# Expert weights in 1 MB chunks of 8 KB runs instead of 2 MB chunks of 16 KB runs

## The reference

```python
def moe_ffn(h, w_router, b_router, w_gu, b_gu, w_down, b_down):
    logits = jnp.matmul(h, w_router, preferred_element_type=F32) + b_router
    top_val, top_e = lax.top_k(logits, TOP_K)              # 4 of 32 experts
    gates = jax.nn.softmax(top_val, axis=-1)
    ...                                                     # tokens sorted by expert
    def expert_block(a):
        xi, e = a
        gate, up = jnp.split(xi @ w_gu[e] + b_gu[e], 2, axis=-1)
        gate = jnp.minimum(gate, SWIGLU_LIMIT)
        up = jnp.clip(up, -SWIGLU_LIMIT, SWIGLU_LIMIT)
        act = (up + 1.0) * gate * jax.nn.sigmoid(SWIGLU_ALPHA * gate)
        return act @ w_down[e] + b_down[e]
    ...                                                     # weighted sum per token
```

## Time and profile before

| What | Value |
|---|---|
| Median of 3 runs | 1431.72 us (1431.07 to 1437.1) |
| Profiled execution, its own time | 1433.07 us |
| Its span (first to last instruction) | 1431.3 us |
| TensorE, busy | 1312.5 us (92%), granted clock 0.982 |
| DVE, ACT, POOL, busy | 437.7, 230.6, 239.6 us |
| Moved by DMA | 482.73 MB, mean 337 GB/s |
| w_gu and w_down | 128 + 64 transfers of 2 MB, 21.9 and 22.4 us from issue to landing (median) |

### The profile page before, as it was taken

One profiled execution on the slowest core, in us unless ns is written; L12 is line 12 of the kernel. 1 busy time (PEld: TensorE's weight loads), 2 busy tenths in 40 slices (PEclk: granted clock), 3 DMA queues, 4 the chain that ended last, 5 costly groups with the idle time before them and its releaser, 6 DMA issues.

```text
span 1431.3 us, 22343 instructions
## 1 busy us (share of the span) xinstructions
PE 1312.5 (92%) x8102; PEld 643.8 (45%) x8102; DVE 437.7 (31%) x853; ACT 230.6 (16%) x537; POOL 239.6 (17%) x477
## 2 busy tenths in 40 slices
PE   7999688999889799999999999998999999899994
PEld 5787565677646333333333333333333333233331
DVE  2124544323431622223232232321232323222226
ACT  1124434120320201001111011110010101100102
POOL 4000000000001312212212122121131221121302
PEclk9999899999999899999999999999999999999997
DMA  9435339525589399999999999999999999999991
GB/s 255 151 106 181 118 115 323 194 101 182 196 331 412 142 394 415 421 415 428 429 431 429 402 425 430 431 430 429 431 419 429 430 430 430 430 424 422 430 430 70
DMA packets 73542, 482.73 MB, mean 337 GB/s; under 512 B 5146, under 2 KB 38098, under 8 KB 48658
## 3 DMA queue, kind: packets, MB, share of 16 engines
q1 hardware_dynamic: 71346, 475.29, 81.6%
q0 software_dynamic: 2064, 6.10, 1.2%
q10 hardware_dynamic: 48, 0.13, 0.0%
HBM read 475.84 MB, written 5.64 MB: 336 GB/s over the span
## 4 chain that ended last, share of the span: by engine, by line
PE 83%; DMA 7%; issue 3%; DVE 3%; ACT 2%; POOL 0%; SPq 0%; ACTq 0%; DVEq 0%; POOLq 0%; PEldq 0%
PE bank L1074 27%; PE bank L546 10%; PE bank L1113 10%; DMA mem<-in_w_gu 5%; PE bank L1023 5%; PE bank L1013 5%; PE bank L555 4%; PE bank L1117 3%; PE bank L533 3%; PE bank L1028 3%; PE bank L967 2%; PE bank L1016 2%; DMA mem<-in_w_in 1%; PE bank L1104 1%; PE bank L1036 1%
## 5 line engine op out<-in xcount | busy, mean ns | idle before, releaser
L1074 PE MATMUL bank<-mem 128*32 128x256 f32 (+1 forms) x3136 | 424.3, 480 | 11.6 <-DMA mem<-in_w_gu 10.4
L1074 PEld LDWEIGHTS bank<-mem 128*32 128x32 f32 (+1 forms) x3136 | 155.7, 121 | 258.9 <-issue 199.6
L2351 DVE TENSOR_TENSOR mem<-mem,bank 128x512 f32<-128x512 f32 (+1 forms) x180 | 114.2, 684 | 406.2 <-PE bank L1013 405.1
L1485 ACT ACTIVATE mem<-bank 128x512 f32<-128x512 f32 (+7 forms) x236 | 110.5, 496 | 549.6 <-PE bank L1113 159.0
L1113 PE MATMUL bank<-mem 128*64 128x512 f32 x672 | 153.5, 598 | 15.4 <-issue 15.4
L546 PE MATMUL bank<-mem 128*128 128x288 f32 (+1 forms) x640 | 158.7, 405 | 4.7 <-PE bank L546 3.3
L546 PEld LDWEIGHTS bank<-mem 128*128 128x128 f32 x640 | 121.4, 192 | 39.9 <-issue 8.4
L1426 POOL COPY mem<-mem 96x64 bf16 x35 | 8.7, 249 | 613.0 <-PE bank L1096 612.7
L1803 ACT ACTIVATE mem<-mem 128x512 f32<-128x512 f32 (+1 forms) x35 | 19.1, 545 | 527.3 <-DVE mem L2365 527.3
L1113 PEld LDWEIGHTS bank<-mem 128*64 128x64 f32 x672 | 48.8, 136 | 90.6 <-issue 90.6
L2285 DVE TENSOR_TENSOR mem<-bank,vec 128x512 f32<-128x512 f32 x36 | 24.9, 692 | 206.0 <-PE bank L1036 206.0
(11 more groups left out here) (248 smaller groups left out, 984.3 us busy)
## 6 DMA issues: line engine op xcount, KB each, us to landing
mem<-in_w_gu SPq DMA_DIRECT2D x128, 2048.0 KB, 21.9
mem<-in_w_down SPq DMA_DIRECT2D x64, 2048.0 KB, 22.4
mem<-in_w_in SPq DMA_DIRECT2D x12, 1024.0 KB, 9.9
mem<-in_w_mkv SPq DMA_DIRECT2D x8, 1024.0 KB, 9.6
mem<-in_cache_k SPq DMA_DIRECT2D x16, 512.0 KB, 7.1
mem<-in_cache_v SPq DMA_DIRECT2D x16, 512.0 KB, 5.5
mem<-in_cache_mem_k SPq DMA_DIRECT2D x8, 1024.0 KB, 4.8
mem<-in_cache_mem_v SPq DMA_DIRECT2D x8, 1024.0 KB, 5.4
```

The lines of the kernel that those rows point to most:

```text
L1074: last = pe.matmul(to, ebias[0:96, 0:kind] if k is None else xgT[:, k, 0:kind], columns(src, j, t, kind), **flags)
L1485: return act.activation(out, in_, ACT.Copy, scale=scale)
L2351: dve.tensor_tensor(a, a, ps, ALU.add).then_inc(added, 1)
```

## The change

Chunks are halved: eight of w_gu (128 rows, one row of 8 KB per partition) and four of w_down (256 rows, two rows per partition), in twenty slots of 1 MB in the same ten places. Both halves of one of the first ten places are issued one behind the other. PE waits for and gives back each half by itself. With one row of w_gu per partition the contraction's blocks are plain blocks of 128 rows, so the reordering around it goes: `gather` reads blocks of 128 columns and has six products of 512 columns in place of four of 512 and four of 256; the second copy of scale and shift with its four transfers goes; narrow passes read and write in one run; the activation's transposes read in another order. `combine` stands behind the fifth block in place of the sixth.

```diff
-GU_CHUNKS, DN_CHUNKS = 4, 2
+GU_CHUNKS, DN_CHUNKS = 8, 4
-ALL = 10
+ALL = 20
-SLOT = 4096
+SLOT = 2048
...
-            at = HOME + PLACES[i % ALL] * SLOT
+            at = HOME + PLACES[i // 2 % len(PLACES)] * 2 * SLOT + i % 2 * SLOT
...
         def gu_src(e, k):
-            return A["w_gu"][0, bass.ds(e, 1), 256 * k:256 * k + 256, :].rearrange("a (p r) n -> p (a r n)", p=P)
+            return A["w_gu"][0, bass.ds(e, 1), P * k:P * k + P, :].rearrange("a p n -> p (a n)")
         def dn_src(e, j):
-            return A["w_down"][0, bass.ds(e, 1), 512 * j:512 * j + 512, :].rearrange("a (p r) n -> p (a r n)", p=P)
+            return A["w_down"][0, bass.ds(e, 1), 256 * j:256 * j + 256, :].rearrange("a (p r) n -> p (a r) n", p=P)
...
-                for c in range(2):
+                for c in range(3):
                     for h in range(2):
-                        pe.matmul(bank[0][64 * h:64 * h + 64, :], pick[:, c, :], z[:, c, :].rearrange("p (q h) -> p h q", h=2)[:, h],
-                                  start=(c == 0), stop=False)
-                for odd in range(2):
-                    for h in range(2):
-                        to = bank[0][64 * h:64 * h + 64, :].rearrange("p (b o x) -> p o b x", b=4, o=2)[:, odd]
-                        last = pe.matmul(to, pick[0:64, 2 + odd, :], z2.rearrange("p (b x h) -> p h b x", b=4, h=2)[:, h],
-                                         start=False, stop=(odd == 1))
+                        if c < 2:
+                            token, rows = pick[:, c, :], z[:, c, :].rearrange("p (b h x) -> p h b x", b=4, h=2)[:, h]
+                        else:
+                            token, rows = pick[0:64, 2 + h, :], z2
+                        last = pe.matmul(bank[0][64 * h:64 * h + 64, :], token, rows, start=(c == 0), stop=(c == 2))
...
-                    if k == 2:
+                    if k == 4:
                         pe.wait_ge(y_ready, n + 1)
                         pe.wait_ge(selT_ready, n + 1)
                         pe.wait_ge(added, n * 5 + 1)
                         combine()
...
-            for name, at in (("ln2_g", 40), ("ln2_b", 48)):
-                for h in range(2):
-                    pool.dma_start(vec_rows[at + 4 * h:at + 4 * h + 4, :], A[name][0].rearrange("(a p h) -> h a p", p=P, h=2)[h],
-                                   allow_slow_non_contiguous=True).then_inc(vec_in, 16)
```

More of the change, by code:

```diff
@@ L190, in chunk_slot @@
         def chunk_slot(i):
-            at = HOME + PLACES[i % ALL] * SLOT
+            at = HOME + PLACES[i // 2 % len(PLACES)] * 2 * SLOT + i % 2 * SLOT
             return mem[:, at:at + SLOT]
         def at_place(place, at, *shape):
-            return carve(mem, HOME + place * SLOT + at, *shape)
+            return carve(mem, HOME + place * 2 * SLOT + at, *shape)
         aT = carve(mem, 0, KB, T)
@@ L1065, in expert_pass @@
                 parts, width = P // kind, D * kind // P
-                def products(src, k, **flags):
+                pe.wait_ge(xg_ready, n + 1)
+                for k in range(KB):
+                    w = chunk_arrived(group, q, k)
                     for j in range(2):
                         for t in range(parts):
-                            to = bank[1 + j][kind * t:kind * t + kind, 0:width]
-                            if kind != CAP:
-                                to = to.rearrange("p (x v) -> p x v", v=2)
-                            last = pe.matmul(to, ebias[0:96, 0:kind] if k is None else xgT[:, k, 0:kind], columns(src, j, t, kind), **flags)
-                    return last
-                pe.wait_ge(xg_ready, n + 1)
-                for k in range(GU_CHUNKS):
-                    w = chunk_arrived(group, q, k)
-                    for r in range(2):
-                        last = products(w[:, 2 * D * r:2 * D * r + 2 * D], 2 * k + r, start=(k + r == 0), stop=(k == GU_CHUNKS - 1 and r == 1))
-                    if k < GU_CHUNKS - 1:
+                            last = pe.matmul(bank[1 + j][kind * t:kind * t + kind, 0:width], xgT[:, k, 0:kind],
+                                             w[:, D * j + width * t:D * j + width * t + width], start=(k == 0), stop=(k == KB - 1))
+                    if k < KB - 1:
                         last.then_inc(chunk_used, 1)
-                    if k == 1:
-                        pe.wait_ge(bias_ready, n + 1)
-                        products(bgu, None, start=False, stop=False)
-                    if k == 2:
+                    if k == 4:
                         pe.wait_ge(y_ready, n + 1)
@@ L1091, in expert_pass @@
                         combine()
+                    if k == 3:
+                        pe.wait_ge(bias_ready, n + 1)
+                        for j in range(2):
+                            for t in range(parts):
+                                pe.matmul(bank[1 + j][kind * t:kind * t + kind, 0:width], ebias[0:96, 0:kind],
+                                          bgu[:, D * j + width * t:D * j + width * t + width], start=False, stop=False)
                 last.then_inc(gu_done, 1)
@@ L1101, in expert_pass @@
                 pe.wait_ge(act_ready, n + 1)
-                by_row = act_s[:, 0:width].rearrange("p (x r) -> p r x", x=P)
+                by_row = act_s[:, 0:width].rearrange("p (i x r) -> p i r x", x=P, r=2)
                 for j in range(width // P):
-                    last = pe.transpose(bank[3][:, P * j:P * j + P], by_row[:, j, :], C("ident"))
+                    last = pe.transpose(bank[3][:, P * j:P * j + P], by_row[:, j // 2, j % 2, :], C("ident"))
                 last.then_inc(act_turned, 1)
@@ L1176, in chunk, with first_chunk @@
                 j = i % CHUNKS_E
-                src = gu_src(e, j) if j < GU_CHUNKS else dn_src(e, j - GU_CHUNKS)
-                sp.dma_start(chunk_slot(i), src).then_inc(slot_in[i % ALL], 16)
-            def first_chunk(i):
-                chunk(i // CHUNKS_E, i)
+                dst, s = chunk_slot(i), slot_in[i % ALL]
+                if j < KB:
+                    sp.dma_start(dst, gu_src(e, j)).then_inc(s, 16)
+                else:
+                    sp.dma_start(dst.rearrange("p (r n) -> p r n", r=2), dn_src(e, j - KB)).then_inc(s, 16)
+            def first_chunk(place):
+                for i in (2 * place, 2 * place + 1):
+                    chunk(i // CHUNKS_E, i)
             for i, item in enumerate(ITEMS):
@@ L1596, in _ @@
             last.then_inc(read_sem(("vs",)), 1)
-            carry(("vec",), vec[:, :], wide(56))
+            carry(("vec",), vec[:, :], wide(40))
             act.wait_ge(keys_stored, 16 * 2)
```

39 lines of the change are left out of this document (18 added, 21 removed).

## The result

| | before | after |
|---|---|---|
| median of 9 runs each on one chip | 1432.32 us (1431.07 to 1437.1) | 1424.95 us (1418.97 to 1426.37) |
| profiled execution (span) | 1433.07 us (1431.3) | 1421.8 us (1420.0) |

The ratio of the two kernels over all these runs is 0.993, with a 95% interval of [0.9915, 0.9946]; that of the two medians is 0.9949. The time of 1424.95 lies in the forecast range of 1424 to 1439, but the forecast was "no change" (1429.5, chance 0.66), and "faster" had 0.14.

A forecast was written before the change was run, and what follows sets the result against it. The expert stage was taken as bound by PE, then the weight stream, then PE. Terms +4.9 - 1.1 - 2.46 - 3.0 - 0.6 = -2.3 us; from the median of 1431.72 the forecast was 1429.5 us, range 1424 to 1439.

The forecast's parts named there:

- the start: Kernel start: four single-word gathers leave the POOL queue, removing PE's 0.58 us wait for first weights; -0.6 us.
- stream, 8 KB runs: Expert weights from 814.86 to 1236.49: 8 KB runs cost 0.059 us more per old chunk, 83 chunks, +4.9 us.
- halves (1.1 and 2.46): Stream-bound piece: earlier return of space near 814.86 saves 1.1 us; PE starting on the first half at its end saves 2.46.
- the combine's place: Expert passes: combine moves one block ahead; its input is ready since the pass before, so nothing new is waited for.
- gather: Next tokens' gather: 0.15 us shorter in thirteen passes before 814.86 and seven behind 1236.49; -3.0 us.
- narrow reading: Narrow experts' products: one run instead of pairs costs nothing, 0.060 us per 256 columns in both.
- issues of SP: Sign of being right: SP issues of 1 MB take about the old time each.
- the stall at 814.86: Expert stage: the stream last found no place here; before it PE alone was taken to set the time.
- The slow stream: Rival, expert weights: 8 KB runs pay the 4 KB price, 0.175 us per chunk; 1439, chance 0.2 with all else slower.
- the transfers in a row: Rival, expert weights: transfers do not overlap, so 2.7 us latency adds to each of 364 halves; 2410, chance 0.01.
- The runs cost nothing: Rival, expert weights: 8 KB runs cost 0 per chunk and the gather gains its best; 1421, chance 0.14.
- The down source: Rival, down weights: runs stay 4 KB there, so the stream costs 8.1 us instead of 4.9; 1432.7, chance 0.05.

The follow-up runs named there:

- words back: Changed kernel with the four single-word gathers of the scale and shift copy issued again at the start, into rows nothing reads: 1427.96 us.
- before, no words: Kernel before the change, only its second scale and shift copy loaded in rows of 1 KB instead of four gathers of single words: 1429.24 us.
- words late: Changed kernel with the four single-word gathers back, but issued behind POOL's last copy of queries: 1422.81 us.
- all back: Changed kernel with start-time single-word gathers, narrow reading in pairs, the former gather, and halves awaited and returned two at a time: 1435.9 us, ratio 1.003 to before.
- pairs of places: Changed kernel, still 1 MB transfers, but TensorE waits for two halves at once and places are given back two at a time: 1429.49 us.
- old-gather: Changed kernel with the next tokens' gather as eight products of 512 columns with stride 2 and eight of 256: 1424.42 us.

## Why the prediction was wrong

It forecast -2.3 us, no change that a measurement can tell, and the medians moved by -7.4. The step that failed worst is the start. In the prediction's words, of the single words: "They share the engines with the first weights, and PE's only wait for those is 0.58 us: -0.6 us". Three pairs of kernels, each kernel set against its own kernel before, give 1.8 (words back against after), 3.2 (before, no words) and 2.7 (words back against words late); by the ratios it is 4.7, 4.0 and 2.7. So it was about 3 us, to within some 2. With 3.0 in place of 0.6 the sum would be -4.7, still under the 7.2 that the prediction could tell: the other terms below had to be off as well, by amounts of which each alone is too small to be told in a median. I took the longest wait in one execution for the bound of the gain. But the wait was short because TensorE came late in that execution: between 12 and 17 us its records of the first product took 663 ns each in the trace before and 410 in the one after, both at a granted clock of 1.00 (why, is open), and it reached the second chunk's products only at 24.1, by which time the chunk was nearly there. In the three other traces with the words it arrived near 21.6 and waited 2.45 to 3.05 us; then the granted clock fell to half, and the 16 records behind the wait took 5.6 to 7.0 us in place of 4.04. What did not depend on that chance was in the profile all along: 195 and 168 GB/s at a share over 1 in a stretch where 383 was shown a moment later, and a landing 20.4 us behind its issue.

The other terms, against the stage:

| term | forecast | measured |
|---|---|---|
| stream, 8 KB runs | +4.9 (0.059 a chunk) | +3.2 (all back against before, the combine's place in it) |
| halves (1.1 and 2.46) | -3.6 | -4.9 (pairs of places) |
| the combine's place | 0 | -1.1 (may be a part of the halves) |
| gather | -3.0 | -1.1 |
| narrow reading | 0 | -0.7 |
| start (by the totals) | -0.6 | about -3 |

- **Stream.** The mechanism and the place were right, the full stretches at 426 as foretold. The 80 steps of 2 MB between the landings of the 160th and the 320th MB took 392.7 us before and 395.4 after: 0.033 us each. The cache stretch at 416 had stood too low as an end of the line; 419 gave 0.046, which the prediction mentioned and did not take. The estimate of 0.028 by the Trainium skill ("DMA: Bandwidth & Descriptors", "Why small descriptors are slow (HBM only)") was nearer to 0.033 than mine was; the 0.046 of the full slices lies between the two. By the same rule 4 KB runs would cost 0.085 us more than 16 KB ones for 2 MB, an estimate, where the full slices give 0.134 and the landings 0.129.
- **Halves.** The mechanism was right, and the gain more than forecast. With them the dip near 815 us disappeared. That "nothing new is waited for" held for the combine, but its place counted all the same: it fills the time until a half lands. One sign failed: issues of SP did not stay at about the old time each (median 1364 ns against 333), without a cost that shows.
- **Gather.** The size per pass was right (0.13 for 0.15), the count was not. I counted thirteen passes ahead of the stall at 814.86 as TensorE's alone. Without that stall the stream is full from about 640 us on (the 80th to the 160th MB land at 4.94 us for 2 MB, its full pace), and a shorter gather ahead of it only lengthens TensorE's wait near 985: of 2.2 us there the old-gather trace gives back 1.9. What pays in full are the six or seven gathers behind the last wait for data. The 1.1 us are eight or nine gathers at 0.13, not twenty.
- **Narrow reading.** "0.060 us per 256 columns in both" compared records of 256 columns in pairs with records of 512 in one run. The records of 512 still take 0.060; those of 256 in one run, which no row of before showed, take 0.057.
- **Rivals.** The slow stream (1439) and the transfers in a row (2410) are out. "The runs cost nothing" (1421) named the right class, faster, for a wrong reason: the runs do cost, and the gain was elsewhere. In time 1421 and the forecast of 1429.5 are about equally far from 1424.95. The down source moves 8 KB runs; otherwise the rate would be lower than 426.

Undone together (all back against after), halves, gather and narrow reading are worth 7.8 us of the stage, and undone singly 4.9 + 1.1 + 0.7 = 6.7. The combine's 1.1 would close that gap, but all back leaves the combine where the change put it, so such a fit is luck: undone parts overlap, and each stage is one execution. Between the traces the stage gained 7.8 - 3.2 = 4.6. With 3 us of the start that makes 7.6, against 7.4 in the medians, 9.4 in the means and 10.0 by the ratio. What stays open is the size of the start term to better than 2 us: the half-clock stretches between 140 and 225 us and near 420 and 475 us fall differently in every trace, and move the start of the second pass from 509.9 to 519.2 us among kernels without the words.

## What to carry to other kernels

A wait in one execution is no bound for what a slow transfer costs; read when the transfer lands and at what rate its engines move while they are called busy. When a kernel changes sides between the stream and an engine, an edit moves the border itself, so count the passes that pay by the border after the edit and not before. Waiting for the weights and giving back their space in halves bought more (4.9 us) than the shorter runs cost (3.2). Transfers of 2 MB in 8 KB runs moved as fast as those of 1 MB, so it is the runs and the waits that are to be weighed, not the number of transfers.

## What was not expected of the hardware

- Four gathers of 512 words of 4 bytes, 8 KB in all, halved the engines' rate from 396 to 195 GB/s for 16 us and put a 1 MB load back by 9 us.
- A transfer into 64 of 128 partitions ran at 216 GB/s at a DMA share of 1.01.
- A TensorE record of 256 columns read in pairs of f32 takes 0.060 us, read in one run 0.057; with 512 columns in stride 2 a record of the gather takes 0.244 (1.95 / 8), in runs 0.239 (2.87 / 12, of which four have 64 rows).
- With ten or eleven transfers of 1 MB on the way, one issue of SP took up to 5.85 us in place of 0.33.
